# A bidirectional RWKV-7 scan: gram and turn products, their evictions and two other operations placed at other steps of the round

## The reference

```
def _wkv7_step(S, inp):
    r_t, w_t, k_t, v_t, aa_t, bb_t = inp
    sa = jnp.einsum('zbhij,zbhj->zbhi', S, aa_t)
    S = S * w_t[..., None, :] + sa[..., :, None] * bb_t[..., None, :] + v_t[..., :, None] * k_t[..., None, :]
    y = jnp.einsum('zbhij,zbhj->zbhi', S, r_t)
    return S, y
...
    seq = tuple(jnp.moveaxis(_flip_bwd(z), 2, 0) for z in (r2, w_h, k_h, v2, aa, bb))
    S0 = jnp.zeros((2, b, N_HEADS, HEAD_DIM, HEAD_DIM), f32)
    _, ys = lax.scan(_wkv7_step, S0, seq)
    y = jnp.sum(_flip_bwd(jnp.moveaxis(ys, 0, 2)), axis=0)
```

## Time and profile before

| | |
|---|---|
| time, median of three runs | 4859.77 us |
| time of the profiled execution | 4860.11 us |
| span of the profiled execution | 4858.3 us |
| share of the span: PE, DVE, ACT, POOL | 88%, 40%, 28%, 27% |
| granted TensorE clock, mean | 0.955 |
| first and last line 1911 of `rwkv_scan` | 2505.9 and 3545.3 us |
| waits of TensorE for line 2003 from 2579 to 3546 us | 77.6 us in 80 |

### The profile page before, as it was taken

How to read it: one execution, slowest core, us unless ns; L and a number is a source line. 1 busy time by engine, 2 the same in 40 slices (tenths; PEclk the granted TensorE clock), 3 DMA queues, 4 the chain that set the end, 5 groups by cost and what they waited for, 6 DMA issues and landing times. The chain is left out here.

```text
span 4858.3 us, 110847 instructions
## 1 busy us (share of the span) xinstructions
PE 4261.1 (88%) x49032; PEld 3567.7 (73%) x49032; DVE 1961.8 (40%) x3539; ACT 1360.7 (28%) x2860; POOL 1290.5 (27%) x794
## 2 busy tenths in 40 slices
PE   3899898999999997996957777777778999999997
PEld 2688856888888885775846676676655888888886
DVE  3011054154152443227137667677643244143441
ACT  1111065211011112236125445555432211111110
POOL 2111032311111114210125555555522311111110
PEclk8899999999999998998979999999999999999998
DMA  4211242311313112221232222212222411312215
GB/s 131 64 55 61 68 134 71 122 40 51 110 40 100 61 58 80 69 78 38 90 86 70 61 74 61 74 57 73 63 97 90 126 35 50 111 40 95 67 48 167
DMA packets 402634, 372.29 MB, mean 77 GB/s; under 512 B 63056, under 2 KB 370512, under 8 KB 399984
## 3 DMA queue, kind: packets, MB, share of 16 engines
q1 hardware_dynamic: 390320, 354.75, 23.7%
q10 hardware_dynamic: 11840, 10.49, 0.6%
HBM read 257.68 MB, written 107.48 MB: 75 GB/s over the span
## 5 line engine op out<-in xcount | busy, mean ns | idle before, releaser
L422 POOL TENSOR_TENSOR f_wlow<-f_raw,f_whigh 128x1024 fp32r<-128x1024 f32 (+1 forms) x152 | 360.2, 2369 | 1670.5 <-ACT f_whigh L493 1670.5
L478 PE MATMUL f_ps<-fx_hh,f_whigh 128*128 128x512 f32 (+1 forms) x2112 | 529.8, 359 | 0.0
L478 PE MATMUL f_ps<-fx_hl,f_whigh 128*128 128x512 f32 (+1 forms) x2112 | 529.0, 358 | 0.0
L478 PE MATMUL f_ps<-fx_hh,f_wlow 128*128 128x512 f32 (+1 forms) x2112 | 528.5, 358 | 0.0
L493 ACT ACTIVATE f_whigh<-f_raw 128x1024 fp32r<-128x1024 f32 (+1 forms) x152 | 156.6, 1030 | 922.4 <-PE f_ps L478 895.3
L478 PEld LDWEIGHTS f_ps<-fx_hl,f_whigh 128*128 128x128 f32 x2112 | 349.1, 189 | 65.3
L478 PEld LDWEIGHTS f_ps<-fx_hh,f_wlow 128*128 128x128 f32 x2112 | 348.9, 189 | 65.4
L478 PEld LDWEIGHTS f_ps<-fx_hh,f_whigh 128*128 128x128 f32 x2112 | 349.1, 189 | 65.0
L478 PE MATMUL f_ps<-mo_oh,f_whigh 128*128 128x512 f32 (+1 forms) x1440 | 361.1, 359 | 25.5 <-POOL f_wlow L422 25.5
L478 PE MATMUL f_ps<-mo_ol,f_whigh 128*128 128x512 f32 (+1 forms) x1440 | 360.4, 359 | 0.0
L478 PE MATMUL f_ps<-mo_oh,f_wlow 128*128 128x512 f32 (+1 forms) x1440 | 359.8, 358 | 0.0
(11 more groups left out here) (267 smaller groups left out, 8278.9 us busy)
## 6 DMA issues: line engine op xcount, KB each, us to landing
f_xo<-xres SPq DMA_DIRECT2D x64, 640.0 KB, 4.0
xres<-f_xo SPq DMA_DIRECT2D x56, 640.0 KB, 3.0
f_raw<-in_ffn_w_gate SPq DMA_DIRECT2D x44, 512.0 KB
f_raw<-in_ffn_w_up SPq DMA_DIRECT2D x44, 512.0 KB
sc_rk<-rkvl SPq DMA_DIRECT2D x80, 256.0 KB, 3.2
rkvl<-ri_ot SPq DMA_DIRECT2D x28, 640.0 KB, 2.9
f_raw<-in_ffn_w_down SPq DMA_DIRECT2D x32, 448.0 KB
qkv_raw<-in_na_w_qkv SPq DMA_DIRECT2D x24, 512.0 KB, 5.6
```

What stands on the lines that cost most here:

```text
L422: nc.gpsimd.tensor_tensor(wlow[:, m % 2, 0:kt], raw[:, 0:kt], whigh[:, m % 2, 0:kt].bitcast(F32), ALU.subtract).then_inc(cut_lo, 1)
L478: last = nc.tensor.matmul(ps[:, m % 2, n, 0:count], w[:, m % 2, k], x[:, k, t0:t0 + count], start=(k == 0 and w is whigh and x is xh), sto ...
```

## The change

Work is moved between steps; none is added or taken away.

- TensorE: the first half of `gram(I+2, 1, ...)` moves from step 6 to step 3, the second from step 7 to step 6. `turn(I+1, 0, ...)` moves from steps 8 and 9 to steps 7 and 8. `turn(I+1, 1, ...)`, both halves at step 10 before, has one half at step 9 and one at step 10.
- ScalarE: `rate_tanh` of step 3 is queued behind `p_copy` of that step instead of ahead of it; `turn_copy(I+1, 0)` moves from step 9 to step 8.
- VectorE: `gram_out`, `inclusive_out` and `inverse_init` of direction 1 move from steps 7, 8 and 10 to steps 6, 7 and 9, and `bonus_rows` moves from step 7 to step 10, directly behind the last level.

```
-                        if n in (6, 7) and group(I + 2):
-                            gram(I + 2, 1, n - 6)
+                        if n in (3, 6) and group(I + 2):
+                            gram(I + 2, 1, n // 3 - 1)
                         if n in (4, 5) and group(I - 1):
                             y_products(I - 1, n - 4)
-                        if n in (8, 9) and group(I + 1):
-                            turn(I + 1, 0, n - 8)
-                        if n == 10 and group(I + 1):
-                            turn(I + 1, 1, 0)
-                            turn(I + 1, 1, 1)
+                        if n in (7, 8) and group(I + 1):
+                            turn(I + 1, 0, n - 7)
+                        if n in (9, 10) and group(I + 1):
+                            turn(I + 1, 1, n - 9)
...
-                        if n == 3 and group(I + 3):
-                            rate_tanh(I + 3)
                         p_copy(I + 1, n)
                         if group(I) and part == 1:
                             fade_state(4 * I + s)
                         if n == 2 and group(I + 3):
                             decay_tanh(I + 3)
                         if n == 3 and group(I + 3):
+                            rate_tanh(I + 3)
                             decay_gate(I + 3)
...
-                        if n == 9 and group(I + 1):
+                        if n == 8 and group(I + 1):
                             turn_copy(I + 1, 0)
...
-                        if n == 7 and group(I + 3):
+                        if n == 6 and group(I + 2):
+                            gram_out(I + 2, 1)
+                        if n == 7 and group(I + 2):
+                            inclusive_out(I + 2, 1)
+                        if n == 9 and group(I + 2):
+                            inverse_init(I + 2, 1)
+                        if n == 10 and group(I + 3):
                             bonus_rows(I + 3)
-                        if n == 7 and group(I + 2):
-                            gram_out(I + 2, 1)
-                        if n == 8 and group(I + 2):
-                            inclusive_out(I + 2, 1)
-                        if n == 10 and group(I + 2):
-                            inverse_init(I + 2, 1)
```

## The result

The changed kernel takes **4927.5 us**, the median of four runs between 4918.42 and 4933.73, against 4859.9 us for the kernel before (four runs). The ratio is 1.0136, with a 95% interval of 1.0117 to 1.0153: slower by 68 us. The forecast was 4888 with a range to 4916. The sign was right, the size was not. The profiled execution took 4932.54 us with a span of 4930.8 us, 72.5 us more than that of before.

A forecast was written before the change was run, and what follows sets the result against it. No engine is full: TensorE sets the pace early in a round, and VectorE is awaited late. A round of 27.35 us plus 0.20 for gaps, against 26.84, adds 26 us over 36 rounds, ends some 3: 4888 us, range 4866 to 4916.

The forecast's parts named there:

- Step 3, the new wait: TensorE's moved gram products must wait for VectorE's `inclusive_out`: it stands 1.85 us, where it stood 0.30 before.
- Steps 3 and 4, the tanh: ScalarE's tanh, queued behind the delayed `p_copy`, holds up TensorE's `y_products`, which come 2.6 us later.
- Steps 4 to 9: The 2.6 us pass on to GpSimd's chain; VectorE's shorter queue leaves TensorE's step 9 only 1.3 us late.
- The block of `bonus_rows`: Step 10: GpSimd's long operation holds up `bonus_rows` until 0.55 us after its end; the state update comes 1.35 us later.
- The gaps: TensorE's "issue" gaps, from `y_products` on, shrink with the added rests: 0.2 us a round instead of 0.84.
- The rival in which they stay: TensorE's "issue" gaps are not cured by rest: 28.19 us a round, 4911 us; chance 0.17.
- The ends: The four rounds at the ends, with part of the new order, add some 3 us, bounded by nothing and 10.
- The rival without a block: `bonus_rows` in step 10 takes 0.71 us unhindered, state update 0.25 us late: 26.45 us a round, 4846 us; chance 0.06.
- the sum itself: 27.35 + 0.20 - 26.84 = 0.71 us a round, times 36 = 26 us, plus some 3 us at the ends.

The follow-up runs named there:

- e7: The changed kernel with `rate_tanh` of step 3 put back ahead of `p_copy`: 4879.9 us, 1.0032 of the kernel before.
- e9: The kernel before with only `rate_tanh` of step 3 moved behind `p_copy`: 4876.8 us, 1.0009 of the kernel before.
- e2: The changed kernel with `bonus_rows` reading its second factor from PSUM, leaving one input in SBUF: 4869.3 us, 1.0009 of the kernel before.
- e4: The kernel before with only `bonus_rows` moved, from step 7 to step 9: 4865.8 us, 1.0006 of the kernel before.
- e1_filled: The changed kernel with three unread products ahead of the step 3 wait and three ahead of the `bonus` wait in step 11: 4888.2 us, 1.0051 of before.
- e8_after_tb7: The changed kernel with `bonus_rows` back at step 7: 4883.9 us, 1.0041 of the kernel before.
- e10_combo: The changed kernel with the first gram half at step 5, `rate_tanh` ahead of `p_copy` and `bonus_rows` at step 8: 4832.2 us, 0.9912 of before.
- e5: The kernel before with only `bonus_rows` moved, from step 7 to step 8: 4844.2 us, 0.9959 of the kernel before.
- e6_tb10_alone: The kernel before with only `bonus_rows` moved, from step 7 to step 10, behind `inverse_init`: 4893.3 us, 1.0058 of the kernel before.

## Why the prediction was right in sign and wrong in size

- **Step 3, the new wait**: right. 1.86 us in each of 36 rounds, forecast 1.85.
- **Steps 3 and 4, the tanh**: right. `y_products` waits 1.04 us on average (1.11 in the round read) and comes at 10.24 us, forecast 10.16. (The overlap of 0.15 us that the working takes from ScalarE's rows is more than the 0.1 us called normal ahead of it; the rows have it.) That the two moves multiply one another, as e7 against e9 shows, was in the working (the copy waits for the delayed inverse level) and is confirmed.
- **Steps 4 to 9**: right within 0.1 us. The 2.6 us reach line 1886, and the wait for the state update falls; at step 9 it is 0.2 us on average, 1.1 before, and the forecast had "a few tenths".
- **The block of `bonus_rows`**: right and shown. It ends 0.55 us after line 2076, e2 removes the 1.0 us by one input in PSUM, e4 stretches it to 3.38. The Trainium skill's rule, cited in the forecast from "SBUF — State Buffer", section "Who interferes with whom", agrees: one SBUF input gave 0.74 us at the same place.
- **The gaps**: right in direction. They fell from 64.2 to 25.4 us, and the rounds at full clock take 27.50, forecast 27.55. The rival in which they stay is refuted. Their cause was left open; it is read below.
- **The ends**: a little low. 7.6 us lie outside the 36 rounds, in e1_filled 8.3; the forecast had 3 with a bound of 10.
- **The rival without a block**: its state update is 0.32 us late by its own terms (3007.7 + 0.71 - 0.08), not 0.25, and it leaves out the ends, some 5 us together. This decides nothing.
- **The step that failed is the sum itself.** It priced each rest of TensorE by what it delays, at a clock taken as given, and under "The gaps" it even booked the added rests as a gain. The term left out is the clock that they cost: 28.64 less 27.50 is 1.14 us a round, 41 us over 36 rounds, and with it 28 becomes 69 of the 72.5 us. e1_filled shows it: the same chain of waits with products in two of the rests has clock 1.00 and a round of 27.48. It takes 4888 us, or 1.0051 of before.

The cause of the gaps stands in the traces' records of transfers. A queue marked "instruction" (for the whole execution: packets, MB, busy share of the DMA engines, before) moves packets of 16384 bytes.

```profile
q8 instruction: 387, 6.34, 0.6%
```

In the 36 rounds before these are 213, one for about 250 products and weight loads of TensorE, and e1_filled, with its extra products, has 217. That the queue is TensorE's is read from these counts. All 63 gaps before and all 37 after end 1.2 to 1.6 us after such a packet landed, each behind another packet. In the 14 traces 850 of 851 gaps end 1.1 to 1.7 us after a landing. That position makes up 13% of the time, and 15% of TensorE's other waits end in it, about what chance gives. So in a gap TensorE waits for its own instructions. A packet never starts less than 3.2 us after the one before, and a round needs six. This fits a dense stretch that outruns its supply and a rest that lets it catch up. It also fits the totals: 16.7 us of gaps in e8_after_tb7, where the other waits are 229 us in all, and 90.3 in e10_combo, where they are 85.

The Trainium skill ("Runtime: NRT & Kernel Launch", section "Instruction fetch mechanics"), on which the rival leaned, has this cost mostly hidden. Here 150 of the 213 packets before have no gap behind them, but in e10_combo only 101 of 214. So the forecast's remark that "hidden" does not hold was not proven when it was made, and is now shown for the 63 packets that have a gap behind them. That the gaps keep a round from getting much below 26.8 us, theory B of e4 and e5, is refuted by e5 and e10, which do.

The row that should have warned was within reach. The 36 rounds before stand at 0.99, not 1.00, and four of them, with all of the 13.7 us at 1.2 GHz, take 28.09 us where the other 32 take 26.68. The forecast put the whole 0.84 us between its gapless round and the mean down to gaps, when 0.16 of it was clock, and so took the clock for something settled. No row of before said how near the clock was to falling further. But those four disturbed rounds were a price: 1.41 us over the others, and had the changed order put that on every round, the forecast's 28 us would have become 79. A rival with the clock so affected would have held the time that was measured. The Trainium skill has the pattern ("TensorE: Matmul & The Clock Gate", section "A second HAM failure mode: psum-queue depth-cycling"): a kernel whose TensorE is idle briefly but often between groups of products can lose its clock again and again, though no single pause is long. Here the trace agrees, with no wait over 2.3 us and a clock of 0.93; it was not weighed in the forecast. The length of a single pause does not tell: the kernel before has a longer one (3.0 us, a gap ahead of line 1702) and a clock of 0.99.

## What to carry to other kernels

A wait added on the engine that sets the pace has two prices: the delay, and the clock that the rest may cost; read how far below 1.00 the stage already stands, and give a forecast with new rests a case in which the clock falls. When a kernel is slower than its chain of waits explains, compare its rounds at full clock with the others (in e6_tb10_alone they are alike, and the clock is not what costs), and fill the rests with products that nobody reads: if it gets faster, it was the clock. A short VectorE operation with two SBUF inputs belongs in front of a long GpSimd operation, not under it, and one that another engine awaits does not belong at the end of a round.

## What the runs showed of the hardware beyond that

- Doing more was faster: about 53 us more of TensorE's busy time made the stage 42 us shorter (e1_filled against after). The changed kernel lost them over 136.5 us at 1.2 GHz, 0.3 us for each. That price is not fixed: in e6_tb10_alone the 30 rounds that share 102.5 us at that level are only 0.04 us longer than the others.
- TensorE's gaps put down to "issue" were waits for its instructions: 850 of 851 ended 1.1 to 1.7 us after a packet of them had landed. There are most of them in the densest order, 90.3 us in e10_combo.
- The VectorE operation that is shut out by GpSimd ended 0.55 to 0.56 us after it in each round read, whatever GpSimd's operation was (lines 2058, 2076 and 2078), which lets its end be worked out from the other engine's row.
- Moving one operation by one step of the order changed the kernel in either direction: `bonus_rows` at step 7, 8, 9 and 10 of the kernel before gives 1, 0.9959, 1.0006 and 1.0058.
